# A hybrid encoder layer on one core: row blocks of 1, 2, 3 and 2 tiles, gathers of 32 tokens by 4 experts, and shorter score and routing steps

## The reference

```python
xn = rmsnorm(x); z = xn @ w_in                     # 1024 x 8192: conv B, C, h | q | k | v | 2 gates
a = (B * dwconv3_causal(C * h)) @ w_conv_out
q, k = rope(rmsnorm(q)), rope(rmsnorm(k))          # 8 heads x 2 components x 64
s = q . k * 64**-0.5, visible up to the end of the query's chunk of 64
o = (softmax(s1) - lam * softmax(s2)) @ v;  o = rmsnorm(o) * 0.8
x = x + (sigmoid(gA) * a + sigmoid(gB) * (o @ w_attn_out)) @ w_o
# routing: 8 heads, two sets of 128 keys, the 16 best of the 16 x 16 sums of the two sets' 16 best
q = rmsnorm(xn2 @ wq); s = q . subkeys; best, e = top 16 of top16(s0) + top16(s1)
g = softmax(best)
x = x + sum over the row's 128 experts of g * gelu(u[e] . xn2) * v[e]     # u, v: 16384 x 1024
```

## Time and profile before

| | |
|---|---|
| runs | 3984.15, 3985.5, 3986.57 us |
| median | 3985.5 us |
| span of the profiled execution | 3979.7 us, 5.8 below that median |
| PE busy | 3171.9 us, 80% |
| DVE busy | 2654.8 us, 67% |
| ACT busy | 1461.1 us, 37% |
| POOL busy | 1531.1 us, 38% |
| DMA | 1340.72 MB, mean 337 GB/s |
| mean granted TensorE clock | 0.872 of full speed |

### The profile page before, as it was taken

One profiled execution on the slowest core, in us unless ns is written; L12 is line 12 of the kernel. 1 busy time (PEld: TensorE's weight loads), 2 busy tenths in 40 slices (PEclk: granted clock), 3 DMA queues, 4 the chain that ended last, 5 costly groups with the idle time before them and its releaser, 6 DMA issues.

```text
span 3979.7 us, 46667 instructions
## 1 busy us (share of the span) xinstructions
PE 3171.9 (80%) x14264; PEld 1436.6 (36%) x14264; DVE 2654.8 (67%) x6242; ACT 1461.1 (37%) x4359; POOL 1531.1 (38%) x1405
## 2 busy tenths in 40 slices
PE   6999988788987999797788887876879666666655
PEld 3555545333433554353333333544425211111110
DVE  3443016988888964778677876885568864556664
ACT  2222001355654244223456564233323333333332
POOL 2111002355655433434445554442344443444333
PEclk9999999889998999898899988888889776776676
DMA  4223336799999999988789999999999999999998
GB/s 157 97 92 102 101 122 257 266 354 340 408 365 387 416 417 392 403 342 342 293 333 375 377 352 397 416 362 368 400 420 404 370 420 420 420 420 419 411 394 346
DMA packets 257065, 1340.72 MB, mean 337 GB/s; under 512 B 31472, under 2 KB 70128, under 8 KB 121392
## 3 DMA queue, kind: packets, MB, share of 16 engines
q0 software_dynamic: 152400, 1108.54, 69.3%
q1 hardware_dynamic: 79344, 204.15, 14.0%
q10 hardware_dynamic: 25072, 25.04, 1.8%
HBM read 1310.49 MB, written 27.15 MB: 336 GB/s over the span
## 4 chain that ended last, share of the span: by engine, by line
PE 42%; DMA 24%; DVE 17%; ACT 6%; issue 4%; DVEq 3%; SPq 2%; ACTq 1%; POOL 1%; POOLq 0%
DMA ringx<-in_peer_uv,tl_idx 12%; DMA mix<-in_peer_uv,tl_idx 11%; PE tl_ps L939 9%; PE tl_ps L991 8%; PE tl_ps L775 6%; PE tl_ps L974 4%; PE tl_ps L923 3%; PE tl_ps L950 3%; PE tl_ps L840 3%; DVE ringx L1610 3%; DVE mix L1610 3%; PE tl_ps L753 2%; DVE tl_xa L1621 2%; PE tl_ps L809 2%; SPq L611 1%
## 5 line engine op out<-in xcount | busy, mean ns | idle before, releaser
L701 POOL DMA_INDIRECT mix<-in_peer_uv,tl_idx x528 | 626.0, 1186 | 782.9 <-PE tl_ps L991 432.8
L701 POOL DMA_INDIRECT ringx<-in_peer_uv,tl_idx x528 | 612.7, 1160 | 731.7 <-PE tl_ps L991 450.8
L1610 DVE CUSTOM_DVE_ANT_0 mix<-mix,tl_xb 128x1024 f32<-128x1024 f32 x528 | 640.9, 1222 | 296.2 <-DMA mix<-in_peer_uv,tl_idx 288.3
L1610 DVE CUSTOM_DVE_ANT_0 ringx<-ringx,tl_xb 128x1024 f32<-128x1024 f32 x528 | 640.7, 1222 | 277.8 <-DMA ringx<-in_peer_uv,tl_idx 270.1
L991 PE MATMUL tl_ps<-ringx,tl_dg 64*64 64x512 f32 x3352 | 569.7, 764 | 298.8 <-ACT tl_dg L1235 298.3
L991 PE MATMUL tl_ps<-mix,tl_dg 64*64 64x512 f32 x3288 | 566.9, 775 | 280.3 <-ACT tl_dg L1235 256.7
L1224 ACT ACTIVATE tl_hg<-tl_hd 128x1 f32<-128x1 f32 x1056 | 213.3, 202 | 1560.9 <-DVE tl_hd L1610 1545.8
L939 PE MATMUL tl_ps<-tl_xr,low 128*128 128x384 f32 (+1 forms) x1280 | 401.9, 470 | 32.2 <-DMA low<-in_wall 27.7
L1228 ACT ACTIVATE tl_hw<-tl_hg,tl_gw 128x1 f32<-128x1 f32 x1056 | 310.9, 294 | 76.1 <-issue 4.6
L991 PEld LDWEIGHTS tl_ps<-ringx,tl_dg 64*64 64x64 f32 x3352 | 105.6, 155 | 639.4 <-ACT tl_dg L1235 566.8
L991 PEld LDWEIGHTS tl_ps<-mix,tl_dg 64*64 64x64 f32 x3288 | 104.9, 157 | 617.8 <-ACT tl_dg L1235 512.6
(11 more groups left out here) (193 smaller groups left out, 4002.1 us busy)
## 6 DMA issues: line engine op xcount, KB each, us to landing
low<-in_wall SPq DMA_DIRECT2D x240, 512.0 KB, 7.9
low<-in_watt SPq DMA_DIRECT2D x60, 512.0 KB, 9.0
mix<-in_peer_uv,tl_idx POOLq DMA_INDIRECT x528, 13.6
ringx<-in_peer_uv,tl_idx POOLq DMA_INDIRECT x528, 13.6
ringx<-in_watt SPq DMA_DIRECT2D x12, 512.0 KB, 5.9
tl_u<-in_x_prompt SPq DMA_DIRECT2D x8, 512.0 KB, 11.8
x_rows<-tl_u SPq DMA_DIRECT2D x8, 512.0 KB, 8.1
xs_rows<-tl_u SPq DMA_DIRECT2D x8, 512.0 KB, 7.5
```

Of the source, the lines that this page charges most:

```text
L701: nc.gpsimd.indirect_dma_start(out=ring[q % RING].rearrange("p a d -> p (a d)"), out_offset=None, in_=A["peer_uv"], in_offset=bass.Indirec ...
L1610: nc.vector.tensor_tensor_reduce(out=ring[q % RING][:, 0, :], in0=ring[q % RING][:, 0, :], in1=xb[:, t % 2, :], scale=1.0, scalar=0.0, op0 ...
```

## The change

The algorithm and its results stay. What is done otherwise:

- **Blocks.** Four row blocks of 1, 2, 3 and 2 tiles (+ 32 sample rows). All dense weights are read four times: 80 blocks of 512 KB more of the shared ring and 24 of the heads' weights. The first slot comes after one tile's dense work. A convolution block for one tile has 128 columns, and the three of a head lie at three positions of the head's seven (CV).
- **Slots.** A slot now serves 32 tokens with four experts each: partition 32 b + i holds the b-th of four experts of token i. Slots form 45 passes (PASSES) of 32 (tile 0: of 8). A pass loads its 32 rows (result rows and normed rows) once, and ACT copies them to the other three quadrants (135 copies). Indices and gates of a unit are brought into that layout by 16 + 16 small DVE copies (`by_quadrants`), or 4 + 4 for the sample rows.
- **Weighing.** The diagonal is 128 x 32, the four matmuls take all 128 rows of v and 256 of its columns each into one quadrant of 32 partitions, and DVE adds a pass's sums to the rows once (`add_sums`). All slots are weighed by TensorE: no row additions, no SHARED.
- **Scores.** -1/8 is put into the query gains once, so the maximum becomes a minimum and needs no scaling; the exponential has scale -1. The mask is added by a matmul over 64 columns for each component instead of a memset. One reciprocal of two sums is left; POOL works the other factor into its own small chain with one more operation.
- **Routing.** The heads of a unit are chosen together, step by step.
- **Queues and tables.** The heads' results are stored from SP's queue and no longer from ACT's. ATT, PLAN and UNIT_AT have new numbers. By them block 0's middle ends at slot 8.4, and the stages of the others are: attention 12 to 56.8, middle 57 to 96; attention 130 to 228, middle 237 to 365; attention 401.9 to 549.5, middle 560 to 729. The units of tile 1 lie at 99.5 to 119.

```diff
-BLOCKS = ((0, 3 * P, (0, 1, 2)), (3 * P, 3 * P, (3, 4, 5)), (6 * P, 2 * P + DEC, (6, 7, 8)))
+BLOCKS = ((0, P, (0,)), (P, 2 * P, (1, 2)), (3 * P, 3 * P, (3, 4, 5)), (6 * P, 2 * P + DEC, (6, 7, 8)))
-ATT = ((-330, 1.0), (25.5, 0.75), (337, 0.93))
+ATT = ((-330, 1.0), (12.0, 0.32), (130.0, 0.5), (401.9, 0.753))
-PLAN = ((-106.5, 1600, 1600, 7), (172.5, 1, 1750, 7), (520, 1, 1100, 7))
+PLAN = ((-106.5, 530, 1481, 2.5), (57.7, 1, 5167, 2.5), (236.6, 1, 2146, 4.0), (558.9, 1, 1278, 5.8))
-SHARED = ((0,170,1,6),(170,300,3,4),(336,520,1,6),(520,680,2,3))
+def place(q):
+    t, k = divmod(q, SLOTS)
+    if t == 0:
+        return t, k // 8 % QUAD, k // 32 * 8 + k % 8
+    return t, k // TOKS, k % TOKS
...
 def weigh(q):
-    for b, h in quarters:
-        rows = half_of(b)
-        last = nc.tensor.matmul(ps[half_of(h), b, :], dg[rows, npe(q) % DIAGS, :],
-                                ring[q % RING][rows, 1, h * 512:(h + 1) * 512], start=k == 0,
-                                stop=t == NT and k == DEC - 1, skip_group_check=True)
+    for b in range(QUAD):
+        last = nc.tensor.matmul(sums(g, b), dg[:, q % DIAGS, :], ring[q % RING][:, 1, b * COLS:(b + 1) * COLS],
+                                start=j == 0 and g < 2, stop=j == TOKS - 1, skip_group_check=True)
...
+def add_sums(q):
+    dve.wait_ge(s["used_pe"], q + 1)
+    nc.vector.tensor_tensor(xa[:, g, :], ps[:, g % 2, g // 2 * COLS:(g // 2 + 1) * COLS], xa[:, g, :], ALU.add)
...
 def score(g, i, components):
+    last = nc.tensor.matmul(scores(t, n, c)[:, key_count(t) - CHUNK:key_count(t)], early[rows[c], :], late[rows[c], :],
+                            start=False, stop=True, skip_group_check=True)
 def row_max(g, i, components):
-    nc.vector.memset(sc[0:CHUNK, nk - CHUNK:nk], LOW)
-    dve.drain()
-    nc.vector.tensor_reduce(mx[:n, w % 2, c:c + 1], sc[:, 0:nk], AX.X, ALU.max)
-    dve.drain()
-    nc.vector.tensor_scalar(nb[:n, w % 2, c:c + 1], mx[:n, w % 2, c:c + 1], -QKS, None, ALU.mult)
+    nc.vector.tensor_reduce(nb[:n, w % 2, c:c + 1], scores(t, n, c)[:, 0:nk], AX.X, ALU.min)
...
+def by_quadrants(dst, src, t, h0, nh):
+    for g in range(1 if t == NT else QUAD):
+        for b in range(QUAD):
+            nc.vector.tensor_copy(dst[quadrant(b), t % 2, first:first + n], src[quadrant(g), b * n:(b + 1) * n])
```

More of the change, by code:

```diff
@@ L196, in _, with pass_length, sums_done @@
                 last.then_inc(s["tr_done"], 1)
-def by_dve(q):
+def place(q):
     t, k = divmod(q, SLOTS)
[L202 to L214, removed]
+    if t == 0:
+        return t, k // 8 % QUAD, k // 32 * 8 + k % 8
+    return t, k // TOKS, k % TOKS
+def pass_length(t):
+    return 8 if t == 0 else TOKS
+PASSES = [(k, 0, k // 8 % QUAD) for k in range(0, SLOTS, 8)] + [(k, k // SLOTS, k % SLOTS // TOKS) for k in range(SLOTS, NT * SLOTS + TOKS, TOKS)]
+PASS_AT = {first: p for p, (first, t, g) in enumerate(PASSES)}
+def sums_done(t, g):
+    return QUAD * t + g + 1
 def plan(rb):
@@ L580, in _ @@
             attend(0)
-            for rb in range(PASSES):
+            for rb in range(NB):
                 tiles = BLOCKS[rb][2]
@@ L717, in norms @@
             def norms():
[L718 to L719 removed]
+                for e in range(REST):
+                    n = rows_of(TILES[0] + e)
                     yield norm_at(e, 5)
@@ new lines, in keep_heads @@
+                    act.wait_ge(s["tq_d"], unit(g, i) + 1)
+                    if i == 0 and old >= 0:
+                        act.wait_ge(s[f"kt_out{old % 2}"], stored_turned(old))
+                    nc.scalar.copy(qTh[:, at:at + n], ps[:, 6, 0:n])
+                    nc.scalar.copy(kTown[:, at:at + n], ps[:, 6, P:P + n]).then_inc(s["tq_c"], 1)
+                units = DC * TILES[rb]
+                for u in range(-3, units + 1):
+                    g, i = place_of(rb, u)
+                    t = tiles[i]
+                    here = 0 <= u < units
+                    if u > 1:
+                        yield step_at(rb, u, TQ + 0.5)
+                        keep_out(*place_of(rb, u - 2))
+                    if 0 <= u + 1 < units:
+                        yield step_at(rb, u, TQ + 0.5)
+                        keep_heads(*place_of(rb, u + 1))
@@ L1318, in choose, with pick_pairs, drop_pairs @@
-                dve.drain()
-                nc.vector.max_index(pick[:, slot, 8:16], best[:, slot, 8:16], cand2[:])
+            def pick_pairs(heads, half):
+                for h in heads:
+                    nc.vector.max_index(pick[:, h, 8 * half:8 * half + 8], best[:, h, 8 * half:8 * half + 8], pairs(h))
+            def drop_pairs(heads):
+                for h in heads:
+                    nc.vector.match_replace(pairs(h), best[:, h, 0:8], pairs(h), LOW)
                 dve.drain()
@@ L1441, in rotate @@
                 def rotate(g, i):
-                    n, j, half = rows_of(tiles[i]), 3 * g + i, HD // 2
+                    n, j, half = rows_of(tiles[i]), unit(g, i), HD // 2
                     dve.wait_ge(s["sq_d"], j + 1)
@@ L1508, in attend @@
+                units = DC * TILES[rb]
+                for u in range(-3, units + 1):
+                    g, i = place_of(rb, u)
+                    t = tiles[i]
+                    here = 0 <= u < units
+                    if rb == 0 and u > 0 and i == 0:
+                        yield step_at(rb, u, CV[2] + 1.8 - PERIOD)
+                        conv_taps(g - 1)
                     if here:
-                        yield step_at(rb, h, base + MX)
+                        yield step_at(rb, u, MX)
@@ L1628, in _ @@
             nc.vector.drain().then_inc(s["setup"], 1)
-            steps = [started(norms())] + [started(part(rb)) for rb in range(PASSES) for part in (attend, middle)] + [started(routing())]
+            steps = [started(norms())] + [started(part(rb)) for rb in range(NB) for part in (attend, middle)] + [started(routing())]
             for q in range(START, 0):
```

932 lines of the change are left out of this document (474 added, 458 removed).

## The result

Slower. The changed kernel takes 4178.48 us (median of 4 runs, 4176.05 to 4185.47) where the kernel before, on the same chip, takes 3984.82; the ratio is 1.0489, 95% interval [1.0474, 1.0504]. The forecast was 3949 us in a range of 3800 to 4110: wrong in sign, and outside the range by 68 us. The profiled execution has a span of 4175.8 us, 233 over the 3943 of the sum.

A forecast was written before the change was run, and what follows sets the result against it. No single bound: TensorE before slot 0, DMA gathers in the last slots, DVE, TensorE or DMA by stage between. Stage times summed to a 3943 us span; with 5.8 us from span to median, 3949 us, range 3800 to 4110.

The forecast's parts named there:

- The step that failed: POOL, each attention unit: one more small operation of 0.5 us ahead of gathers, covered by POOL being half busy.
- Rival 2: Attention of blocks 1 and 2: a unit's chain of engine waits keeps 12.8 us periods; +94, 4043 us; chance 0.13.
- four engines level: I take 190: Block 1's attention, slots 12 to 57: TensorE 163, DVE 165, ACT about as much, DMA 150; taken as 190 us.
- its 330 for block 2: Block 2's attention, slots 130 to 228: TensorE 314, DVE 286, DMA 290; taken as 330 us.
- The routing stage: Slots 97 to 130: 2.3 routing units of 21 us and 33 dots of 1.3, DVE 92, taken as 96 us.
- nothing in sum: Routing units: choosing heads together saves some 2 us, 32 small copies cost 2.9 us, so no net change.
- Rival 1: Weighing on TensorE: strips don't run abreast, 1.21 us in pairs (4081) or 2.07 singly (above 4400); chance 0.20.
- its allowance for the turn: Middles of blocks 1 and 2: the turn raises 324 to 340 us and 552 to 570 us.
- Rival 4: TensorE: narrow matmuls no cheaper, held to a 0.19 us weight load; block 0 costs 92 us more, 4040; chance 0.05.
- The first dot: Block 0, before slot 0: dense work for one tile brings it near 285 us, from 650.
- Rival 3: All stages: each lasts only as long as its busiest engine, nothing lost between engines; 3802 us; chance 0.22.
- The frame of the sum: Whole kernel: a shorter wait before slot 0 pays only if its work gets cheaper later; 365 us off, some 330 back.

The follow-up runs named there:

- e1_no_drain: The changed kernel with a semaphore wait instead of POOL's drain in each attention unit: 4013.05 us, ratio 1.0084 to the kernel before.
- e3_before_drain: The kernel before with a POOL drain added in each attention unit, behind the addition of EPS: 4112.38 us, ratio 1.0324.
- e8_drain_block2_only: e1_no_drain with the drain kept in the 24 attention units of block 2 alone: 4077.99 us.
- e6_pace_block2: e1_no_drain with block 2's attention over 88 slots instead of 98 and its middle over 138 instead of 128: 4018.25 us.
- e7_row_max_as_before: e1_no_drain with the old score step: memset of the mask and multiplication on DVE, each behind a drain, no mask matmul: 4011.37 us.
- e5_pace_block1: e1_no_drain with block 1's attention over 56 slots instead of 45 and its middle over 27 instead of 38: 4024.7 us.
- e4_old_blocks: e1_no_drain with the kernel before's row blocks of 3, 3 and 2 tiles and mostly its tables: 3977.55 us, ratio 0.9991 to the kernel before.

## Why the prediction was wrong

- **The step that failed** is the sentence "POOL gets one more small operation a unit (0.5 us), ahead of gathers; it is half busy." The operation takes 0.4 us; the drain behind it, which the sum put at nothing, stops POOL for 7.9 us each time beside gathers, until the gathers on its own queue have landed, and holds the factor that DVE waits for. POOL's busy share was no cover: during the drain POOL is idle by the profile and yet issues nothing. Price: 165 us of the 233, shown by e1_no_drain, and again by e3_before_drain and e8_drain_block2_only. No row of before could show it, since there no drain of POOL lay beside a gather; but the profile of the kernel before has a gather at 13.6 us from issue to landing, and 64 drains of at most that are 0 to 870 us, an estimate that would have reached over the result. The description of the change does not name the drain either.
- **Rival 2 was partly right.** Without the drain the forecast's "four engines level: I take 190" for block 1 (227) and its 330 for block 2 (359) are still short by 37 and 29 us. Rival 2 had 256 and 358, and 4043 in all for 4013. Its figure for block 2 fits, and e6_pace_block2 shows that the slots do not set that stage; but e7_row_max_as_before shows that not every wait in the unit's chain counts, and in block 1 the period is 11.4 us, under the floor of 12.8, and grows with the slots (e5_pace_block1). That a chain of waits is the cause there is argued, not shown.
- **The routing stage** (96 us forecast, 113 measured) left out a term: the last query blocks' top searches on DVE (L1350 to L1361), 13 us. DVE is busy 103 of 113 us there. The small copies of `by_quadrants` were mis-sized as well: they start 0.18 us apart and not 0.09, so those of a unit of four heads cost 5.7 us and not 2.9, and "nothing in sum" does not hold. From e1_no_drain's routing stage, with two such units:

```profile
L1420 DVE COPY tl_idx<-tl_chosen 32x16 uint32<-32x16 uint32 x32 | 5.8, 181 | 0.5
```

- **Rival 1 fell.** The four strips run abreast. In the TensorE timeline of block 1's middle a weighing takes 0.64 us by itself, and 0.77 out of the dense matmuls' time: dense instructions start 0.216 apart, the last of the first group at 708.32, so the next would start at 708.54; it starts at 709.20, and its successor another 0.1 late. Over 22 weighings of the stage the median is 0.77; by the same count a weighing of the kernel before takes 1.22.

```profile
702.07 6.64 PE L1029 MATMUL tl_ps<-tl_xr,low 128*128 128x256 f32 x30
708.63 0.64 PE L1080 MATMUL tl_ps<-mix,tl_dg 128*32 128x256 f32 x8
709.20 7.17 PE L1029 MATMUL tl_ps<-tl_xr,low 128*128 128x256 f32 x32
```

  The forecast was 0.79. The estimate by the Trainium skill ("TensorE: Matmul & The Clock Gate", "Measured speedup vs the span model"), 0.89 us, is further off here. The middles of blocks 1 and 2 are 16 and 15 us under the forecast; the weighing explains some 4 of these 31, the sum without its allowance for the turn (324 and 552) is nearer.
- **Rival 4 fell too**: 32 instructions of 256 columns take 7.17 us, 0.22 each, and 16 of 128 columns in block 0 take 1.95 us, 0.11 each after the tail. The first dot at 299 us, 14 late, is something else: a whole pass of weights now serves one tile, and TensorE waits before slot 0 for weights, 14.0 us in all, where the kernel before never did. The merge (172.8 to 238.6) takes 66 us for the 55 of the sum, at a DMA share of 0.93, and behind such a wait 16 instructions take 2.84 us for 1.95.

```profile
PE tl_ps L923 <- DMA low<-in_wall: 8.7, 3, 3.5
PE tl_ps L1029 <- DMA low<-in_wall: 5.3, 2, 4.2
209.10 2.84 PE L1029 MATMUL tl_ps<-tl_xr,low 128*128 128x128 f32 x16 [4.17 <-DMA low<-in_wall]
```

- **Rival 3**, every stage at its busiest engine, was far too cheap in the attentions: 165, 314 and 486 us where 227, 359 and 525 are left without the drain.
- **The frame of the sum held**: an early start is worth only what it held is done cheaper later. Without the drain 354 us come off the start and 385 are given back. The blocks of 1, 2, 3 and 2 tiles with their tables cost 35 us net (e4_old_blocks). All the rest of the change without the drain, the removal of 289 us of row additions on DVE among it, is worth nothing together. No run takes the row additions alone; in block 1's middle, with 85 of them, their removal gave TensorE 26 us more to do and the stage became 19 us longer.

## What to carry to other kernels

A drain on an engine that also issues transfers may be no small operation: on POOL here a semaphore did the same for 165 us less. Read such an engine's queue (its drain records, idle time put down to "issue") and not its busy share. Price every synchronising instruction that a change adds by what may be in flight on that engine's queue, not by what it orders, and look for whoever waits for the result behind it. Work that is moved off an engine is worth something only in stages that this engine bounds: 99 us less of DVE in a middle bound by TensorE, and 14 us more in an attention, did not shorten the one or lengthen the other.

## What the hardware showed that was not expected

POOL's drain lasted until its indirect transfers had landed. POOL stood for 7.9 us each beside gathers; the record took 0.3 to 1.4 us while only SP's transfers were under way, and a second drain behind it 0.04 us. Drains on DVE, which issues none of these transfers, showed nothing of the kind: e7_row_max_as_before adds two to each component (medians of 0.24 and 0.83 us, the longest 3.9) and costs no time. And 8 us without a new gather cost the end only some 2.7 us each, with the dots short of gathered data for hardly more time than before; what the kernel lost by the drain it lost, by the waits, on the one small factor behind it.
